# The last output-gate slot leaves the levels of a gated recurrence: its two halves go between the key transposes and the state products

## What is computed

```python
def hgrn2_mixer(z, lb, onorm_g):            # z columns [q | f | i | g]
    q = silu(q) * HG_KDIM ** -0.5
    fg = lb + (1 - lb) * sigmoid(f)
    k, logf, v = 1 - fg, log(fg), i
    # chunk by chunk, per head, b = cumsum(logf):
    o = (q * exp(b)) @ state + (decayed, causal q k^T) @ v
    state = state * exp(b_last) + (k * exp(b_last - b))^T @ v
    return rms_norm(o, onorm_g) * silu(g)
```

## Time and profile before

| what | value |
|---|---|
| median of 3 runs | 2021.27 us (2018.52 to 2023.82) |
| the profiled execution's own time | 2019.51 us |
| its span, first to last instruction | 2017.6 us |
| mean granted TensorE clock | 0.964 |
| TensorE matmul busy | 1925.6 us, 95% of the span |
| VectorE, ScalarE, GpSimd busy | 45%, 37%, 36% |

### The profile page before, as it was taken

One profiled execution on the slowest core, in us unless ns is written; L12 is line 12 of the kernel. 1 busy time (PEld: TensorE's weight loads), 2 busy tenths in 40 slices (PEclk: granted clock), 3 DMA queues, 4 the chain that ended last, 5 costly groups with the idle time before them and its releaser, 6 DMA issues.

```text
span 2017.6 us, 23955 instructions
## 1 busy us (share of the span) xinstructions
PE 1925.6 (95%) x9213; PEld 1531.7 (76%) x9213; DVE 901.0 (45%) x1343; ACT 751.7 (37%) x986; POOL 726.0 (36%) x218
## 2 busy tenths in 40 slices
PE   7999989999999999989899999998989999999988
PEld 5799964788888886636478888887777778878776
DVE  5235654355553125454335555301724754413463
ACT  4142143355554223453335555422322552221423
POOL 2254720344343443600034434344223334344231
PEclk9989986999999999979799999999998999999999
DMA  7531110222322232400022222223213113232221
GB/s 270 228 125 64 42 43 0 84 86 101 104 83 86 100 110 84 146 0 1 0 84 87 100 104 84 86 100 126 77 49 74 43 63 102 99 104 84 83 84 42
DMA packets 28661, 173.21 MB, mean 86 GB/s; under 512 B 2992, under 2 KB 5296, under 8 KB 11440
## 3 DMA queue, kind: packets, MB, share of 16 engines
q1 hardware_dynamic: 25200, 154.15, 22.1%
q10 hardware_dynamic: 3392, 18.09, 2.7%
HBM read 170.13 MB, written 2.10 MB: 85 GB/s over the span
## 4 chain that ended last, share of the span: by engine, by line
PE 46%; issue 38%; POOL 9%; DVE 5%; ACT 1%; POOLq 0%; DVEq 0%; ACTq 0%
PE ps L360 26%; POOL wlo L933 9%; PE ps L682 6%; PE ps L573 2%; PE ps L752 1%; PE ps L758 1%; DVE scr L1838 1%; PE ps L854 1%; PE ps L864 1%; PE ps L837 1%; PE ps L750 1%; PE ps L866 1%; PE ps L865 1%; PE ps L635 1%; DVE scr L2031 1%
## 5 line engine op out<-in xcount | busy, mean ns | idle before, releaser
L933 POOL TENSOR_TENSOR wlo<-wraw,whi 128x2048 fp32r<-128x2048 f32 (+1 forms) x153 | 660.9, 4319 | 1223.2 <-ACT whi L1016 1205.3
L360 PE MATMUL ps<-hh,whi 128*128 128x512 f32 x1383 | 543.4, 393 | 8.2 <-DVE hl L1421 4.5
L360 PE MATMUL ps<-hl,whi 128*128 128x512 f32 x1383 | 539.4, 390 | 0.0
L360 PE MATMUL ps<-hh,wlo 128*128 128x512 f32 x1383 | 539.2, 390 | 0.0
L1016 ACT ACTIVATE whi<-wraw 128x2048 fp32r<-128x2048 f32 (+1 forms) x149 | 269.8, 1811 | 448.2 <-PE ps L360 355.4
L360 PEld LDWEIGHTS ps<-hh,whi 128*128 128x128 f32 x1383 | 260.3, 188 | 67.5 <-issue 5.8
L360 PEld LDWEIGHTS ps<-hh,wlo 128*128 128x128 f32 x1383 | 260.3, 188 | 54.5
L360 PEld LDWEIGHTS ps<-hl,whi 128*128 128x128 f32 x1383 | 260.4, 188 | 54.1 <-issue 0.7
L1716 DVE SCALAR_TENSOR_TENSOR scr<-ps,vec,scr 128x510 f32<-128x510 f32 (+1 forms) x176 | 120.2, 745 | 93.1 <-ACT scr L1210 93.1
L682 PE MATMUL ps<-gh,whi 128*128 128x512 f32 x352 | 137.1, 390 | 1.3 <-DVE gl L1731 1.3
L682 PE MATMUL ps<-gl,whi 128*128 128x512 f32 x352 | 136.9, 389 | 0.0
(11 more groups left out here) (387 smaller groups left out, 2851.8 us busy)
## 6 DMA issues: line engine op xcount, KB each, us to landing
wraw<-in_w SPq DMA_DIRECT2D x95, 1024.0 KB, 4.9
wraw<-in_w0b SPq DMA_DIRECT2D x26, 1024.0 KB, 4.9
wraw<-in_wd SPq DMA_DIRECT2D x32, 704.0 KB, 4.1
ada<-in_wada ACTq DMA_DIRECT2D x12, 1024.0 KB, 7.0
xtok<-in_x SPq DMA_DIRECT2D x4, 512.0 KB, 8.0
out<-ytok SPq DMA_DIRECT2D x2, 1024.0 KB, 4.2
wbias<-in_rpb ACTq DMA_DIRECT2D x8, 192.0 KB, 7.4
mtok<-in_mem ACTq DMA_DIRECT2D x1, 1024.0 KB, 7.0
```

Of the source, the lines that this page charges most:

```text
L360: last = mm(o, l, r, start=(k == 0 and n == 0), stop=(k == K - 1 and n == 2))
L933: nc.gpsimd.tensor_tensor(wlo[:, s % 2, 0:wd], wraw[:, s % 2, 0:wd], whi[:, s % 2, 0:wd].bitcast(F32), ALU.subtract).then_inc(lo_ready, 1)
```

## The change

Halves 0 to 5 (slots 13 to 15) stay behind levels 0 to 5. Nothing stands behind levels 6 and 7 any more. Half 6 comes behind the key transposes of heads 0 and 1, half 7 behind those of heads 2 to 5, ahead of the state products. On ScalarE the high part of slot 18 moves behind the six copies of transposed keys. On VectorE the last slot is taken out behind the wait for the last totals, ahead of the copy of the chunks' decays and of the state updates. No instruction is added or removed.

```diff
--- before.py
+++ after.py
@@ -560,6 +560,15 @@
 
             pe.wait_ge(g_dve, 3)
             pe.wait_ge(emptied, S_Z0B + 3)
+            def gate_half(k):
+                s, b = S_Z0B + 3 + k // 2, k % 2
+                if b == 0:
+                    pe.wait_ge(emptied, s)
+                    pe.wait_ge(lo_ready, s + 1)
+                last = three(ps[:, 6 + b, :], wv(s % 2, 256, off=b * P), hv_(), 8)
+                if b:
+                    last.then_inc(used, 1)
+
             for k in range(8):
                 for hf in range(2):
                     if k:
@@ -572,13 +581,8 @@
                             t = slice(c * P, (c + 1) * P)
                             last = mm(ps[:, h, t], hk[:, h, t], hq[:, h, t], start=True, stop=True)
                     last.then_inc(lv_mm, 1)
-                s, b = S_Z0B + 3 + k // 2, k % 2
-                if b == 0:
-                    pe.wait_ge(emptied, s)
-                    pe.wait_ge(lo_ready, s + 1)
-                last = three(ps[:, 6 + b, :], wv(s % 2, 256, off=b * P), hv_(), 8)
-                if b:
-                    last.then_inc(used, 1)
+                if k < 6:
+                    gate_half(k)
 
             pe.wait_ge(lv_cp, 16)
             for n in range(HH):
@@ -588,6 +592,9 @@
                 for c in range(3):
                     last = nc.tensor.transpose(ps[:, n % 2, c * P:(c + 1) * P], hk[:, n, c * P:(c + 1) * P], cc("ident"))
                 last.then_inc(st_tr, 1)
+                if n == 1:
+                    gate_half(6)
+            gate_half(7)
             for n in range(HH):
                 pe.wait_ge(st_tc, n + 1)
                 if n >= 2:
@@ -1127,10 +1134,10 @@
             A(hq[:], hq[:], ACT.Silu).then_inc(g_act, 1)
             for s in range(S_Z0B + 2, S_O0 + 1):
                 conv_upto(s)
-            conv_upto(S_O0 + 1)
             for n in range(HH):
                 act.wait_ge(st_tr, n + 1)
                 A(hkT[:, n, 0:3, :], ps[:, n % 2, 0:3 * P].rearrange("p (c k) -> p c k", k=P), ACT.Copy).then_inc(st_tc, 1)
+            conv_upto(S_O0 + 1)
             act.wait_ge(emptied, S_O0)
             A(hgate[:], hgate[:], ACT.Silu).then_inc(g_act, 1)
             nc.scalar.preload_act_table_set("natural_log_exp_and_others")
@@ -1591,10 +1598,11 @@
                     src = ps[:, 3 * hf:3 * hf + 3, :].rearrange("p a t -> p (a t)").rearrange("p (c g t) -> p c g t", c=12, t=2 * h)[:, :, :, h:2 * h]
                     dst = hA[:, 3 * hf:3 * hf + 3, :].rearrange("p a t -> p (a t)").rearrange("p (c g t) -> p c g t", c=12, t=2 * h)[:, :, :, h:2 * h]
                     V.copy_predicated(dst, msk.unsqueeze(1).to_broadcast([P, 12, n, h]), src).then_inc(lv_cp, 1)
-                if k % 2:
+                if k in (1, 3, 5):
                     take_z0(S_Z0B + 3 + k // 2)
 
             dve.wait_ge(lv_t, 14)
+            take_z0(S_O0 - 1)
             link(V.tensor_copy(chunk_decay.rearrange("p (h c) -> p h c", c=4), hb[:].rearrange("p h (c t) -> p h c t", t=P)[:, :, :, P - 1]))
             for n in range(HH):
                 dve.wait_ge(st_kv, n + 1)
```

## The result

The changed kernel takes 2027.47 us (median of 11 runs, 2024.67 to 2032.81), the kernel before 2021.65 (11 runs, 2018.52 to 2023.82). The ratio of the mean times is 1.0033 with a 95% interval of 1.0023 to 1.0044: slower, by 6.7 us with 4.6 to 8.9 in the interval; the medians lie 5.8 us apart. Forecast were 2027.8 us and 0.32%.

A forecast was written before the change was run, and what follows sets the result against it. TensorE was taken to bound the kernel, never leaving the chain of waits from 185.04 to 260.81 us. Dependencies +4.4 and clock losses +2.1 gave +6.5 us on 2021.27: 2027.8 us, range 2022.3 to 2032.0.

The forecast's parts named there:

- gap ahead of level 7, ended by GpSimd's `hk`: Between levels 6 and 7, TensorE idles 3.55 us until GpSimd's multiply of `hk`, delayed by slot 17's low part, ends.
- level 7 for the clock: In level 7, TensorE's clock likely falls behind the 3.55 us gap, costing 1.2 us, between 0 and 1.86.
- end of level 7 to the transposes: Behind level 7, key transposes wait 2.07 us for VectorE's last masked copy, which half 7 no longer covers.
- heads 0 and 1 with half 6, for the clock: Behind the 2.07 us gap, a possible clock fall during these transposes and half 6 costs 0.9 us, between 0 and 1.86.
- end of half 7 to the first update: Ahead of the state updates, VectorE's last-slot take and decay copy set the start, 1.45 us; the state product needs only 0.94.
- stretch against before: From level 0's products to VectorE's first state update: 4.4 us of dependencies plus 2.1 of clock loss, +6.5 us.
- The levels: In the levels, gate halves fill TensorE's waits; without half 6, level 7 starts 1.90 us earlier, not 5.46.
- The dependencies' part: From level 7 to the first state update, 17.11 us replace 10.79: +6.32, less 1.90 for level 7's earlier start, +4.42 us.
- The clock's part: TensorE's clock falls behind the two new gaps, costing 1.2 and 0.9 us, together 2.1, between 0 and 3.7.
- The rule on transposes: At the second gap, transposes not counting as busy would make the clock's fall sure: +7.5 us, 2028.8; chance 0.08.
- Rival: no clock loss: Both new gaps pass without a clock fall: +4.4 us, 2025.7, within 0.3%; chance 0.15.
- Rival: memory attention at the high clock: From 309 to 329 us, shifted matmuls run at the high clock, saving 7.5 us: 2020.3; chance 0.10.

The follow-up runs named there:

- filled: Changed kernel with TensorE kept busy in both gaps by six products nobody reads, against the kernel before: 2023.29 against 2022.07 us, ratio 1.0014.
- the split take: Changed kernel with VectorE taking half 6 out of PSUM as soon as it is done, leaving only half 7's multiply for later: one run, 2023.09 us.
- the low part late: Changed kernel with GpSimd's low part of slot 17 done behind the levels, against the kernel before: 2019.93 against 2022.07 us, ratio 0.9995.

## Why the prediction was right, step by step

| step | forecast, us | profile after, us |
|---|---|---|
| gap ahead of level 7, ended by GpSimd's `hk` | 3.55 | 3.50 |
| level 7 for the clock | +1.2 (0 to 1.86) | +1.5 (9.07 to the transposes, against 7.58 filled) |
| end of level 7 to the transposes | 2.07 | 1.97 |
| heads 0 and 1 with half 6, for the clock | +0.9 (0 to 1.86) | +1.58 (7.78 against 6.20) |
| end of half 7 to the first update | 1.45 | 1.69, counted from the first state product's row |
| stretch against before | +6.5 | +7.84 |

- **The levels.** That the halves are cover and not load is shown from both sides: with the low part out of the way the gap vanishes in the changed kernel, and the kernel before doesn't notice. That level 7 starts less than 2 us earlier for 5.46 us of work taken away was right to 0.05 us. What the forecast left out is VectorE's copy 0.46 us ahead of GpSimd; it changed nothing here.
- **The dependencies' part**, 4.42, was measured at 4.76 with the clock held high. Of the difference 0.24 is the last step: from the start of the first state product to the first update it is 1.69 and not 0.94, so the take costs 0.75 us and not 0.51. The forecast counted that step from VectorE's row (266.29) where the other steps run from start to start of TensorE's rows; there the next row starts at 266.10. The rest, 0.14, lies between level 7 and the transposes (7.58 in the filled kernel against 5.37 + 2.07).
- **The clock's part**, 2.1, was the least certain term. It was 3.1 (by the filled gaps) in the profiled execution and 1.6 in the profile with the split take. The first fall came in each of three profiles and cost 1.5 to 1.6, more than the 1.2 taken. The second came in two of four, at 1.6 and 1.0 us; their mean, 0.65, is an estimate over four different kernels, and the 0.9 taken stands for no single execution. It wasn't counted that the kernel before loses 0.6 us in some executions as well: of the three profiles with the old order on ScalarE, the one in the earlier trace rows is the only one in which the clock stayed at 1.00 there.
- **Luck in the total.** The stretch grew by 7.84 us and not 6.5, and the time by 6.7 (5.8 by the medians). That the forecast of the time is closer than that of the stretch isn't its doing: nothing in it gives back the rest.
- **The rule on transposes** of the Trainium skill (TensorE: Matmul & The Clock Gate, Part 4: PE-mode transpose), by which the forecast made the second fall sure, isn't borne out as a certainty: with the split take and in the changed kernel with the low part late, the same gap of 1.98 us, followed by the same transposes, passed at 1.00. That transposes do less to hold the clock than products stays possible: the clock fell behind waits and transposes in two of the three profiles with the old order on ScalarE, and no run here tries products in their place. Where the fall came in the changed kernel it cost 1.58.
- **Rival: no clock loss.** It would have given +4.4. The filled kernel is that case: +4.76 in its profile, +2.8 us in time.
- **Rival: memory attention at the high clock.** It didn't come. From 314 to 344 us the clock stood at 0.50. The time from the first state update to the next low part on GpSimd (355.27 before, 363.45 after) is 85.67 us after and 83.67 before; in the second profile of the kernel before it is 86.45. In the five other profiles of kernels made from the changed one it is 82.35 to 83.95. If the change gives something back in this stage, it would explain why the times of half 7 alone, of the low part late and of the filled gaps lie 1.3 to 2.1 us below their stretches; one profile of each doesn't show it.
- **A stage far behind.** From that low part to the end of the span the changed kernel's profile is 3.8 us shorter (1658.5 against 1662.3) with the same instructions. Nearly all of it lies between two roundings of slots on ScalarE: 163.34 us before (845.12 to 1008.46) and 159.72 after (853.39 to 1013.11), at a mean granted clock of 0.83 and 0.85 over the first 159 us. In the eight other profiles this piece takes 162.8 to 163.5 us. So the profiled execution had a gain there that none of the others had, and it is the fastest of its eleven. What sets the clock there wasn't tried.
- **What moved and cost nothing.** ScalarE idled 3.24 us ahead of its first square, 3.91 before: the Silu was in time. GpSimd idled 80.63 us ahead of its next low part.

The half-moves measure the price of each half: half 6 +3.4, half 7 +2.5 in the profiles, 5.9 together and 7.84 when both are moved. Both half-moves contain the gain of about 1.5 us of ScalarE's new order, the full change only once: 5.9 + 1.5 = 7.4, and the second clock loss was larger in the full change (1.58 against 1.0), which comes within 0.2 us of the 7.84.

## What to carry to other kernels

If the chain of waits runs on TensorE through a stretch, filler work between dependent steps is what hides the other engines' latencies; taking it out gives back only what those engines let through, here 1.9 us for 5.5 us of work, and the work must still be done elsewhere. Count what every gap uncovers before moving the filler, and then add the clock: behind the gap of 3.5 us it cost 1.5 to 1.6 us more each time, behind that of 2 us between nothing and 1.6. Follow the wait that a gap uncovers to its start, too: here it began with half 5, whose end lets ScalarE round, then GpSimd subtract. When a change has several parts, price each: one line of this one, the order on ScalarE, was worth 1.5 us of stretch by itself, and the others cost 9.3 us (7.84 + 1.46), six times as much.

## What the runs showed of the hardware

- The same gap makes the clock fall in one execution and not in another. The gap of 1.98 us ahead of the transposes was followed by a fall in the changed kernel and with half 7 alone moved, and by none with the low part late or with the split take. The waits of 1.82 and 0.29 us of the kernel before had no fall in its first profile, a fall in its second and one in the profile with the low part late. The gap of 3.5 us was followed by a fall each of the three times, and so was the one of 1.84 us ahead of level 0 in all ten profiles (level 0 took 7.22 us in each).
- With six products that nobody reads in the time of the gaps the clock stayed at 1.00 from 243 to 273 us, and the stretch is 98.54 against 101.62. Against an execution without the second fall (100.15, by the split take) the gain is 1.6 us.
- VectorE's multiply of `hq`, with both operands in SBUF, takes 4.63 us where it runs beside GpSimd's low part of slot 17 and 0.96 where it doesn't (level 6 in the changed kernel and with the low part late). It ended at 250.34, 0.8 us behind the low part. The operations on state products, with one operand in PSUM, took 0.73 us beside the low part of slot 18 and without it.

The two rows are from VectorE's timelines of the changed kernel and of the one with the low part late:

```profile
245.71 4.63 DVE L1595 TENSOR_TENSOR hq<-hq,hb 128x768 f32<-128x768 f32 x1 [1.39 <-PE ps L582]
```

```profile
246.40 0.96 DVE L1596 TENSOR_TENSOR hq<-hq,hb 128x768 f32<-128x768 f32 x1 [1.39 <-PE ps L582]
```
